# Projection pieces, heads and router products in parts between the gathered rows, and one channel block of the long convolution on GpSimd

## The chip, the cores and the metric

The kernel runs on one core of a Trainium2 chip. The metric is the device time of one execution in microseconds, the median of the runs. The core has TensorE (products into PSUM banks), VectorE, ScalarE, GpSimd (which also issues the gathers) and a queue for plain DMAs.

## What is computed

A first block and a second block over 512 tokens of width 1024, all in float32. The first block is cut here to what matters; the second (feed-forward layer, two attention mixers, feed-forward layer) follows on its result.

```python
proj = rms_norm(h, norm_mix_g) @ w_in                 # xv, bg, cg, ga, gg: 5 x 512 columns
y_sc = bg * causal_depthwise_conv(cg * xv, w_conv)    # width 3
u    = causal_depthwise_conv(ga * sigmoid(gg), w_dw) + b_dw   # width 31, 512 channels
y_cf = silu(layer_norm(u, ln_g, ln_b))
h    = h + concat(rms_norm(y_sc), rms_norm(y_cf)) @ w_out
hn   = rms_norm(h, norm_ffn_g)
q    = (hn @ w_q).reshape(512, 8, 256)
s1, s2 = q[..., :128] @ keys[:, 0].T, q[..., 128:] @ keys[:, 1].T   # 8 heads, 128 + 128 scores
# 16 best of each, 16 best of their sums: idx (one of 16384 experts) and gates (softmax), per token and head
h    = h + sum over 8 heads and 16 experts of gelu(u[idx] . hn) * gate * v[idx]
```

The last line reads 512 x 128 expert rows, each 1024 values of u and 1024 of v.

## The kernel before, in words

Tokens are cut in tiles of 128 (tile 0, and "the rest", 384 tokens, REST). The program of each engine is written out by hand, and semaphores order them.

**Prelude.** Tile 0 goes alone through projection, convolutions, output projection and hn (TensorE lines 795 to 831). Then head 0 of the router gives its list (route(0), line 1955), and the rows begin.

**Rows.** The experts are read in 512 "rows" of 1 MB: GpSimd issues for row i one gather into pair[i % 7] (NPAIR is 7, line 2834); VectorE forms the dot products (dot, 2011), ScalarE the weight and a diagonal matrix of it (weigh, 2679), and TensorE adds the weighted v (add_pair, 919, two rows at each odd i below 256) into a bank. v_used then frees the buffers, for which gather i + 7 waits (row_used, 573). The first four buffers' uses are special: gathers 3 to 6 wait for pieces 1, 3, 5 and 7 of the rest's projection, whose weights lie in their buffers. Below row 256 the tokens are arranged as 64 tokens x 2 experts, so each list is permuted by TensorE (permute, 783: indexes and gates in one bank) and copied back by VectorE (lists_back, 1999) before its rows; list r is found at rows up to TOP_ROW[r], permuted at PERM_ROW (TOP + 3) and copied at BACK_ROW (TOP + 5).

**Between rows.** Every engine has generators that yield the row at which a step is due (Paced, 313); the loop calls `until(i)` once a row, behind that row's own work on TensorE, VectorE and ScalarE and ahead of the gather on GpSimd. So the rest is computed beside the gathers: 20 projection pieces (rest_in, 719, eight products of 384 columns each; PIECE_ROW names the row of each), tile 0's heads 2 to 7 (head_q and head_S; Q_ROW), the long convolution, 30 fused multiply-adds of 384 columns for each of four channel blocks on VectorE (conv 1285, pump 1401: two taps at each row with i % 16 >= 4), the output projection from row 56, mean and variance at MEAN = 80 and VAR = 84, hn of tiles 1 to 3 up to row 115, and the router for them in nine calls (call, 896; CALL_ROW), each of sixteen products of 384 columns (128 or 256 for two of them) in one block, and six for the scores.

From row 264 the second block's first half (chain A, paced by clock) runs between the rows; chain B, for tiles 2 and 3, runs alone after row 511. Weights come in pieces of 1 MB into three slots, in the order of ORDER; each waits for the last product of the piece three before it. A bank's next use waits until its previous one is read (fresh, 671, on the counts that Plan lays out; `perm` is bank 1).

## Time and profile before

| | us |
|---|---|
| median of 3 runs | 2448.38 |
| lowest, highest | 2442.33, 2451.57 |
| profiled execution | 2457.3 |
| its span, first to last instruction | 2455.4 |
| TensorE busy | 2063.0 (84%) |
| VectorE busy | 1775.5 (72%) |
| ScalarE busy | 1174.0 (48%) |
| GpSimd busy | 729.2 (30%) |
| mean granted TensorE clock | 0.907 |

Busy time is a sum over stages with different limits, so the stretches are read one by one. A timeline row gives the start and the length of an instruction or of several alike (xN); in brackets stands how long its engine was idle before, and whom it waited for. Each float32 product of TensorE leaves two records. "POOL" is GpSimd, "DVE" VectorE, "ACT" ScalarE, "PE" TensorE.

### The profile page before, as it was taken

To read this page: it belongs to the slowest core of one execution; us is meant where nothing else is said; L and a number is where in the kernel's file an instruction comes from. 1 tells how busy PE (TensorE), PEld (TensorE's weight loads), DVE (VectorE), ACT (ScalarE), POOL (GpSimd) and SP (SyncE) were. 2 spreads that over 40 slices of the span, in tenths; PEclk is the share of its full clock that TensorE was granted. 3 is DMA by queue.
4 is the path that set the end of the run, shared out by engine and by line. 5 is a ranking of instruction groups with operands and counts; after the bars stand their busy time and mean duration, and the time that the engine had idled before them with its cause. 6 is when DMAs were issued, how large, how long until landed. Compare 5 with 4: busy or idle time off the path is not lost. (4 is left out here: it accounts for less than half of the span.)

```text
span 2455.4 us, 29687 instructions
## 1 busy us (share of the span) xinstructions
PE 2063.0 (84%) x9896; PEld 1423.4 (58%) x9896; DVE 1775.5 (72%) x3485; ACT 1174.0 (48%) x3850; POOL 729.2 (30%) x637
## 2 busy tenths in 40 slices
PE   8888886878875556999794678599989999999999
PEld 7544432334331112886343467388639988898997
DVE  6568885556668888888888998866666656656564
ACT  4345455654545556343345655433344435444443
POOL 0123343433343435233356553433320001100000
PEclk9999988889897777999896689799999999999999
DMA  9179999789889999999999999999995554124554
GB/s 363 66 288 389 368 382 376 296 333 369 341 335 383 400 408 406 383 393 421 419 398 367 374 412 420 421 394 419 420 383 189 189 167 171 69 96 162 173 188 137
DMA packets 109768, 777.73 MB, mean 317 GB/s; under 512 B 12320, under 2 KB 13088, under 8 KB 16688
## 3 DMA queue, kind: packets, MB, share of 16 engines
q0 software_dynamic: 73728, 536.90, 54.5%
q1 hardware_dynamic: 35888, 238.93, 25.7%
q8 instruction: 79, 1.29, 0.2%
q14 instruction: 73, 0.60, 0.1%
HBM read 773.69 MB, written 2.10 MB: 316 GB/s over the span
## 5 line engine op out<-in xcount | busy, mean ns | idle before, releaser
L2834 POOL DMA_INDIRECT pair<-in_uv,idx x512 | 610.0, 1191 | 921.1 <-DVE resid L1259 484.3
L2106 ACT ACTIVATE smalls<-smalls 128x1 f32<-128x1 f32 (+1 forms) x2058 | 540.5, 286 | 678.8 <-DVE smalls L2018 658.1
L664 PE MATMUL bank<-pair,diag 128*64 128x512 f32 (+1 forms) x1056 | 338.9, 760 | 208.8 <-ACT diag L2106 207.6
L2018 DVE CUSTOM_DVE_ANT_0 pair<-pair,hd 128x1024 f32<-128x1024 f32 x256 | 311.7, 1221 | 122.0 <-DMA pair<-in_uv,idx 118.7
L664 PE MATMUL bank<-ft,raw 128*128 128x256 f32 x1664 | 372.3, 386 | 11.9 <-DVE ft L1253 11.9
L664 PEld LDWEIGHTS bank<-ft,raw 128*128 128x128 f32 x1664 | 322.3, 195 | 57.7 <-issue 12.6
L2018 DVE CUSTOM_DVE_ANT_0 pair<-pair,hn 128x1024 f32<-128x1024 f32 x256 | 312.5, 1221 | 57.7 <-DMA pair<-in_uv,idx 56.8
L664 PEld LDWEIGHTS bank<-pair,diag 128*64 128x64 f32 (+1 forms) x1056 | 80.4, 163 | 421.6 <-ACT diag L2106 299.6
L1259 DVE SCALAR_TENSOR_TENSOR resid<-pair,smalls,resid 128x1024 f32<-128x1024 f32 x243 | 311.0, 1280 | 0.7 <-ACT smalls L2106 0.6
L1253 DVE TENSOR_TENSOR half<-raw,half 128x1024 fp32r<-128x1024 f32 (+2 forms) x184 | 212.0, 1191 | 122.7 <-ACT half L2106 121.2
L2106 ACT ACTIVATE half<-raw 128x1024 fp32r<-128x1024 f32 (+2 forms) x184 | 179.5, 1023 | 90.9 <-PE bank L664 90.8
L664 PE MATMUL bank<-ft_hi,half 128*128 128x256 f32 x960 | 176.5, 284 | 1.5 <-DVE ft_early L1253 1.5
L664 PE MATMUL bank<-raw,hidden 128*128 128x512 f32 x352 | 151.4, 592 | 0.0
L664 PEld LDWEIGHTS bank<-ft_hi,half 128*128 128x128 f32 x960 | 149.6, 190 | 1.9 <-issue 1.8
L2106 ACT ACTIVATE smalls<-smalls,gat 128x1 f32<-128x1 f32 x512 | 143.1, 280 | 0.0
L664 PE MATMUL bank<-ft_late_hi,half 128*128 128x256 f32 x704 | 127.5, 284 | 2.3 <-DVE ft_late_lo L1253 2.3
L2739 POOL TENSOR_TENSOR smalls<-smalls,mh 128x1 f32<-128x1 f32 (+1 forms) x21 | 18.1, 864 | 357.9 <-DVE smalls L1256 357.7
L664 PE MATMUL bank<-ht,raw 128*128 128x128 f32 (+2 forms) x512 | 117.9, 391 | 2.7 <-ACT scores L2106 2.3
L664 PEld LDWEIGHTS bank<-raw,hidden 128*128 128x128 f32 x352 | 66.9, 190 | 83.3 <-issue 83.2
L664 PE MATMUL bank<-half,hidden_hi 128*128 128x512 f32 x352 | 110.8, 395 | 1.6 <-DVE half L1253 1.6
L664 PEld LDWEIGHTS bank<-ft_late_hi,half 128*128 128x128 f32 x704 | 109.6, 190 | 2.6 <-issue 2.5
L664 PEld LDWEIGHTS bank<-ht,raw 128*128 128x128 f32 x512 | 81.7, 201 | 48.8 <-issue 20.4
(327 smaller groups left out, 3183.3 us busy)
## 6 DMA issues: line engine op xcount, KB each, us to landing
raw<-in_wts SPq DMA_DIRECT2D x201, 1024.0 KB
pair<-in_wts SPq DMA_DIRECT2D x10, 1024.0 KB, 11.0
pair<-in_uv,idx POOLq DMA_INDIRECT x512
raw<-in_wts SPq DMA_DIRECT2D x10, 512.0 KB
raw<-in_wts SPq DMA_DIRECT2D x4, 720.0 KB
resid<-in_x SPq DMA_DIRECT2D x4, 512.0 KB, 11.7
out<-resid SPq DMA_DIRECT2D x8, 256.0 KB, 5.8
raw<-in_wts SPq DMA_DIRECT2D x2, 768.0 KB
```

Source lines behind the costliest of these rows:

```text
L664: return e.matmul(o, a, b, start=start, stop=stop)
L1253: return e.tensor_tensor(o, a, b, op)
L1259: return e.scalar_tensor_tensor(out=o, in0=a, scalar=s, in1=b, op0=op0, op1=op1)
L2018: e.tensor_tensor_reduce(b[:, 0:1024], b[:, 0:1024], x_, 1.0, 0.0, ALU.mult, ALU.add, actv[:, i % 8:i % 8 + 1]).then_inc(dotted, 1)
L2106: return e.activation(o, i, f, **kw)
L2739: e.tensor_tensor(nrs[0:n, c:c + 1], nqs[0:n, c:c + 1], mh[0:n, 0:1], ALU.pow).then_inc(n_rs, 1)
L2834: e.indirect_dma_start(pair[i % NPAIR], None, uv, bass.IndirectOffsetOnAxis(ap=idx[:, n % SLOTS, k:k + 1], axis=0)).then_inc(pairs_in[i % ...
```

## The change

**Pieces and heads in halves.** rest_in(n, part) does four of the eight products; PIECE_ROWS gives each half its row. head_q takes one or both of its halves, at rows Q_ROW and Q_ROW + 1, and head_S follows at Q_ROW + 3. Head 2 moves from before row 0 to rows 7, 8 and 10. Pieces, heads and the rest become three generators of their own on TensorE, heads one on ScalarE.

**Calls in quarters.** A call's sixteen products are issued four at each of four rows; its scores follow at CALL_ROW + 5. Four calls start one or two rows earlier.

**Prelude.** Piece 0 goes in halves around the mean's column sum; the cf part's mean is taken off and squared ahead of the sc part; pieces 1, 2 and 3 are placed later; on VectorE rest_u(0) and the taps (26 before, 8 now) come after hn.

**Permutation.** Indexes and gates are permuted by two calls, each with its own use of bank 1, and VectorE copies each back with one instruction of 128 partitions in place of two of 64.

**Convolution.** VectorE does three of the four channel blocks. GpSimd does the last: for each of 30 taps a product into rstdr and an addition, one operation a row from row 16 to row 75.

**Order of weights.** Piece sc2 comes before head 3's.

```diff
-ORDER = ([(k, 2048) for k in [("wq", 1), ("wq", 2), ("sc", 0), ("sc", 1), ("wq", 3), ("sc", 2), ("sc", 3), ("bg", 0), ("wq", 4),
+ORDER = ([(k, 2048) for k in [("wq", 1), ("wq", 2), ("sc", 0), ("sc", 1), ("sc", 2), ("wq", 3), ("sc", 3), ("bg", 0), ("wq", 4),
...
-PIECE_ROW = [0, 0, 0, 0, 0, 1, 2, 3, 8, 11, 14, 16, 22, 25, 28, 31, 34, 37, 42, 45]
-Q_ROW = {3: 19, 4: 39, 5: 48, 6: 69, 7: 74}
+PIECE_ROWS = [(1, 1), (1, 3), (3, 3), (5, 5), (9, 9), (11, 11), (13, 15), (15, 17), (17, 19), (23, 25), (25, 27), (29, 29),
+              (31, 33), (35, 35), (39, 41), (43, 43)]
+Q_ROW = {2: 7, 3: 21, 4: 37, 5: 47, 6: 69, 7: 74}
...
-CALL_ROW = [104, 118, 124, 129, 136, 142, 150, 158, 166]
+CALL_ROW = [104, 118, 124, 129, 134, 142, 149, 157, 165]
...
-    p.add("perm", [1] * 16)
+    p.add("perm", [1] * 32)
...
-            def rest_in(n):
+            def rest_in(n, part):
...
-                o, done = fresh("R", n)
-                for kt in range(8):
-                    ins = mm(o[:, 0:REST], w[:, kt, j * P:(j + 1) * P], XTR[:, kt, :], kt == 0, kt == 7)
-                ins.then_inc(done, 1)
+                b = B["R", n]
+                if part == 0:
+                    fresh("R", n)
+                for kt in range(4 * part, 4 * part + 4):
+                    ins = mm(bank[b.bank][:, 0:REST], w[:, kt, j * P:(j + 1) * P], XTR[:, kt, :], kt == 0, kt == 7)
+                if part:
+                    ins.then_inc(full[b.bank], 1)
...
-            def head_q(c):
+            def head_q(c, parts=(0, 1)):
...
-                o, done = fresh("q1", c)
-                for s in range(2):
+                b = B["q1", c]
+                for s in parts:
+                    if s == 0:
+                        fresh("q1", c)
                     for kt in range(8):
-                        ins = mm(o[:, s * P:(s + 1) * P], w[:, kt, s * P:(s + 1) * P], HT[:, 0, kt, :], kt == 0, kt == 7)
-                ins.then_inc(done, 1)
+                        ins = mm(bank[b.bank][:, s * P:(s + 1) * P], w[:, kt, s * P:(s + 1) * P], HT[:, 0, kt, :], kt == 0, kt == 7)
+                    if s:
+                        ins.then_inc(full[b.bank], 1)
...
+            def permute(r, m):
+
+                e.wait_ge(gated if m else routed, r + 1)
+                src = gat[:, r % SLOTS, :] if m else ixf[r % 2]
+                o, done = fresh("perm", 2 * r + m)
...
+                    for c in range(2):
+                        ins = mm(o[64 * c:64 * c + 64, 8 * j:8 * j + 8], idt[:, 64 * j:64 * j + 64],
+                                 src.rearrange("p (q e) -> p e q", e=2)[:, c, :], True, True)
...
+            for n in (8, 9):
+                taken(e, "norm0", n)
+            rest_in(0, 0)
             e.wait_ge(late_in, 96)
             e.wait_ge(keys_in, 16)
-            taken(e, "norm0", 8)
-            taken(e, "norm0", 9)
-            rest_in(0)
             e.wait_ge(taps_done, 4)
             colsum("mean", 0, [YT0[:, 4 + ct, :] for ct in range(4)], P)
+            rest_in(0, 1)
+            e.wait_ge(sq_wide, 1)
+            colsum("var", 0, [wide0[0][:, ct * P:(ct + 1) * P] for ct in range(4)], P)
             e.wait_ge(y_hi, 4)
             y_out("ysc", 0, first_weights(10).rearrange("p (k n) -> p k n", k=4), lambda k: YT0[:, k, :], 0)
             e.wait_ge(sq_wide, 2)
-            colsum("var", 0, [wide0[0][:, ct * P:(ct + 1) * P] for ct in range(4)], P)
             mean_squares("ms", 0, [wide0[1]])
             y_out("ysc", 1, first_weights(11).rearrange("p (k n) -> p k n", k=4), lambda k: YT0[:, k, :], 0)
-            rest_in(1)
+            e.wait_ge(sq_wide, 3)
+            mean_squares("mc", 0, [wide0[1]])
             e.wait_ge(y_hi, 8)
             y_out("ycf", 0, first_weights(12).rearrange("p (k n) -> p k n", k=4), lambda k: YT0[:, k, :], 4)
             y_out("ycf", 1, first_weights(13).rearrange("p (k n) -> p k n", k=4), lambda k: YT0[:, k, :], 4)
-            e.wait_ge(sq_wide, 3)
-            mean_squares("mc", 0, [wide0[1]])
-            rest_in(2)
+            rest_in(1, 0)
+            rest_in(1, 1)
...
-            permute(0)
-            head_q(2)
-            head_S(2)
-            rest_in(3)
+            permute(0, 0)
+            rest_in(2, 0)
+            permute(0, 1)
+            rest_in(2, 1)
+            rest_in(3, 0)
+            rest_in(3, 1)
+
+            def pieces():
+
+                for n in range(4, 20):
+                    for part in range(2):
+                        yield PIECE_ROWS[n - 4][part]
+                        rest_in(n, part)
+
+            def heads():
+
+                for c, row in Q_ROW.items():
+                    yield row
+                    head_q(c, (0,))
+                    yield row + 1
+                    head_q(c, (1,))
+                    yield row + 3
+                    head_S(c)
...
+                        if kt % 4 == 0:
+                            yield CALL_ROW[c] + 2 * s + kt // 4
...
-                yield CALL_ROW[c] + 3
+                yield CALL_ROW[c] + 5
...
-            between = Paced(rest())
+            strands = Paced(pieces()), Paced(heads()), Paced(rest())
...
                     if row == i:
-                        permute(r)
-                between.until(i)
+                        for m in range(2):
+                            permute(r, m)
+                for strand in strands:
+                    strand.until(i)
...
+            centred(0, YT0[:, 4:8, :], P)
...
-            taps = [conv(YTR[:, 4 + ct, :], upadr, "cf", 31, ct, 0, REST, 9 + ct, taps_done) for ct in range(4)]
+            taps = [conv(YTR[:, 4 + ct, :], upadr, "cf", 31, ct, 0, REST, 9 + ct, taps_done) for ct in range(3)]
...
-            rest_u(0)
...
-            pump(10)
...
             mean_of("hn", 0)
-            pump(2)
             row_out(0)
-            pump(14)
+            rest_u(0)
+            pump(8)
...
-                        taken(e, "perm", n - 2)
+                        taken(e, "perm", 2 * n - 4)
...
+            def lists_back(r, m):
+
+                o, out_ = filled(e, "perm", 2 * r + m)
+                e.tensor_copy((gat if m else idx)[:, r, :].rearrange("p (q j) -> p q j", j=2),
+                              o[:, 0:16].rearrange("p (j q) -> p q j", j=2)).then_inc(out_, 1)
...
-                            lists_back(r)
+                            for m in range(2):
+                                lists_back(r, m)
...
+            taken(e, "mean", 0)
+            act(wide0[0].rearrange("p (c n) -> p c n", c=4), YT0[:, 4:8, :], ACT.Square).then_inc(sq_wide, 1)
...
-            e.wait_ge(sq_wide, 1)
+            e.wait_ge(sq_wide, 2)
             for ct in range(4):
                 gained(YT0[:, ct, :], "g_sc", ct)
-            taken(e, "mean", 0)
-            act(wide0[0].rearrange("p (c n) -> p c n", c=4), YT0[:, 4:8, :], ACT.Square).then_inc(sq_wide, 1)
             taken(e, "var", 0)
...
-            rest_gate(0)
-            rest_tap(0)
...
                 for s in range(2):
+                    yield CALL_ROW[c] + 2 + 2 * s
...
             row_turned(0)
+            rest_gate(0)
+            rest_tap(0)
             head_q(0)
             head_S(0)
             doubled(0)
             head_q(1)
...
-                        taken(e, "perm", n)
+                        taken(e, "perm", 2 * n + 1)
...
-            head_q(2)
-            head_S(2)
...
+            def last_conv():
+
+                acc, w0 = YTR[:, 7, :], COLS["cf"][0] + 3 * 31
+                yield 16
+                e.wait_ge(first_tap, 12)
+                for j in range(1, 31):
+                    if j > 1:
+                        e.wait_ge(p_step, 2 * j - 2)
+                    e.tensor_scalar(rstdr, upadr[:, 3, j:j + REST], colt[:, w0 + j:w0 + j + 1], 1.0, ALU.mult, ALU.mult).then_inc(p_step, 1)
+                    yield 15 + 2 * j
+                    e.wait_ge(p_step, 2 * j - 1)
+                    e.tensor_tensor(acc, acc, rstdr, ALU.add).then_inc(p_step if j < 30 else taps_done, 1)
+                    yield 16 + 2 * j
...
-            first, between = Paced(chain("A")), Paced(rest())
+            first, strands = Paced(chain("A")), (Paced(last_conv()), Paced(rest()))
...
-                        e.wait_ge(permuted, 3 * n + 2)
+                        taken(e, "perm", 2 * n)
```

## Rows read from the trace of the kernel before

**Rows 1.** The page: DMA busy tenths in 40 slices of the span
```profile
DMA  9179999789889999999999999999995554124554
```

**Rows 2.** Busy time by stretch, all engines, granted clock, DMA share and rate
```profile
core 0: us, PE busy (x) PEld busy (x) DVE busy (x) ACT busy (x) POOL busy (x), PEclk, DMA share, GB/s
160.00:400.00 240.00, 204.51 (x823) 94.49 (x824) 190.72 (x416) 124.53 (x490) 96.90 (x85) 0.89 0.97 387
400.00:530.00 130.00, 90.88 (x344) 36.69 (x344) 85.60 (x191) 78.51 (x275) 52.40 (x49) 0.82 0.83 324
530.00:590.00 60.00, 53.06 (x218) 28.39 (x216) 28.24 (x69) 31.16 (x123) 21.62 (x21) 0.94 0.82 320
590.00:727.00 137.00, 108.20 (x456) 51.71 (x452) 92.48 (x257) 68.14 (x274) 49.04 (x48) 0.90 0.90 354
727.00:960.00 233.00, 131.49 (x389) 32.44 (x386) 196.27 (x529) 135.31 (x560) 105.93 (x95) 0.76 0.99 397
960.00:1840.00 880.00, 736.75 (x2777) 524.68 (x2775) 719.74 (x1183) 393.00 (x1534) 360.79 (x295) 0.89 0.99 402
```

**Rows 3.** The same view of line 2018 alone, the dots
```profile
160.00:400.00 240.00, 91.35 (x149) 0.89 0.97 387
...
590.00:727.00 137.00, 49.33 (x81) 0.90 0.90 354
```

**Rows 4.** Timeline of TensorE: start, length, engine, line, operation [idle before <-releaser]
```profile
87.12 5.41 PE L664 MATMUL bank<-xt_rest,pair 128*128 128x384 f32 x16
...
94.09 1.09 PE L684 MATMUL bank<-idt,hn 128*128 128x128 f32 x8 [1.56 <-DVE hn L1259]
...
163.98 3.66 PE L664 MATMUL bank<-pair,diag 128*64 128x512 f32 x8 [9.58 <-ACT diag L2106]
...
167.44 0.39 PE L664 MATMUL bank<-smalls,idt 128*64 128x16 f32 x8
...
182.61 1.94 PE L664 MATMUL bank<-pair,diag 128*64 128x512 f32 x8
```

**Rows 5.** Timeline of VectorE from 93 to 162 us
```profile
93.95 9.12 DVE L1259 SCALAR_TENSOR_TENSOR yt_rest<-upad_rest,colt,yt_rest 128x384 f32<-128x384 f32 x14
...
103.17 0.29 DVE L1930 MAX8 vals<-scores 128x8 f32<-128x128 f32 x1
...
146.29 1.23 DVE L2018 CUSTOM_DVE_ANT_0 pair<-pair,hd 128x1024 f32<-128x1024 f32 x1 [4.82 <-DMA pair<-in_uv,idx]
...
158.59 1.23 DVE L2018 CUSTOM_DVE_ANT_0 pair<-pair,hd 128x1024 f32<-128x1024 f32 x1 [9.42 <-DMA pair<-in_uv,idx]
...
161.09 1.23 DVE L2018 CUSTOM_DVE_ANT_0 pair<-pair,hd 128x1024 f32<-128x1024 f32 x1
```

**Rows 6.** Timeline of GpSimd from 114 to 153 us
```profile
114.20 0.28 POOL L2798 TENSOR_SCALAR gat<-gat,sm 128x16 f32<-128x16 f32 x1
...
116.34 1.19 POOL L2834 DMA_INDIRECT pair<-in_uv,idx  x1 [1.86 <-DVE gat L2006]
...
140.42 1.21 POOL L2834 DMA_INDIRECT pair<-in_uv,idx  x1 [11.45 <-PE bank L664]
...
152.81 0.94 POOL L2834 DMA_INDIRECT pair<-in_uv,idx  x1 [11.18 <-PE bank L664]
```

**Rows 7.** Timelines of TensorE, GpSimd and VectorE at one call
```profile
642.95 11.76 PE L664 MATMUL bank<-ht,raw 128*128 128x384 f32 x32
...
656.86 0.94 POOL L2834 DMA_INDIRECT pair<-in_uv,idx  x1 [10.42 <-PE bank L664]
...
661.10 0.38 DVE L2006 CAST idx<-bank 64x16 uint32<-64x16 f32 x2 [8.35 <-remote]
```

**Rows 8.** Timeline of all engines at 363 us
```profile
363.37 1.22 DVE L2018 CUSTOM_DVE_ANT_0 pair<-pair,hd 128x1024 f32<-128x1024 f32 x1
...
363.39 2.40 POOL L2798 TENSOR_SCALAR gat<-gat,sm 128x16 f32<-128x16 f32 x1
```

**Rows 9.** Groups by shape: GpSimd, busy us and mean ns of one
```profile
L2763 POOL TENSOR_TENSOR smalls<-smalls,mh 128x8 f32<-128x8 f32 x20 | 38.1, 1914 | 73.7 <-DVE smalls L1256 73.5
```

More of the change, by code:

```diff
@@ L890, in rest @@
                 turned_rows("hn", "hn", 3, HN[3])
-                yield 115
-                doubled(1)
+                for j in range(2):
+                    yield 115 + 2 * j
+                    doubled(1, j)
                 for c in range(1, len(CALLS)):
@@ L2063, in vector @@
                         if row_ == i:
-                            lists_back(r)
+                            for m in range(2):
+                                lists_back(r, m)
                     between.until(i)
@@ L2582, in call, with heads @@
                 for s in range(2):
[L2583 removed]
+                    yield CALL_ROW[c] + 6 + s
                     o, out_ = filled(e, "S3", 2 * c + s)
                     act(S[:, a:b_, 2 * h + s, :], o[:, 0:n].rearrange("p (t n) -> p t n", t=b_ - a), ACT.Copy).then_inc(out_, 1)
[L2587 to L2595 removed]
+            def heads():
+                for c, row in Q_ROW.items():
+                    yield row + 2
+                    head_q(c)
+                    yield row + 4
+                    head_S(c)
+            def rest():
                 for ct, due in ((1, 0), (2, 4), (3, 6)):
@@ L2608, in rest @@
                     rest_sc_tap(ct)
-                yield from singles(33, 52)
                 yield 53
@@ L2619, in rest @@
                     gained(YTR[:, ct, :], "g_sc", ct)
-                yield from singles(52, 80)
                 yield MEAN + 3
@@ L2698, in scalar @@
             gates(0)
-            head_q(2)
-            head_S(2)
-            first, between = Paced(chain("A")), Paced(rest())
+            first, strands = Paced(chain("A")), (Paced(heads()), Paced(rest()))
             for n in range(32):
@@ L2718, in scalar @@
                         final_row(n // 8 - 1)
-                    between.until(i)
+                    for strand in strands:
+                        strand.until(i)
                     first.until(clock(i))
@@ L2809, in rest @@
                         rate("hn", t)
+            def last_conv():
[10 more added lines that the diff above has]
+                    yield 16 + 2 * j
             e.wait_ge(padded, 4)
             gates(0)
-            first, between = Paced(chain("A")), Paced(rest())
+            first, strands = Paced(chain("A")), (Paced(last_conv()), Paced(rest()))
             for i in range(PAIRS):
@@ L2816, in pool @@
                 first.until(clock(i - 8))
-                between.until(i)
+                for strand in strands:
+                    strand.until(i)
                 for r in range(1, SLOTS):
```

75 lines of the change are left out of this document (13 added, 62 removed).

## Prediction

> **What bounds the kernel now.** I read the timeline in slices first. The DMA line [rows 1] is low in slices 2 and 3 (61 to 184 us), has 7s and 8s among its 9s up to slice 12 (737 us), only 9s up to slice 30, and 1s to 5s after. Then the stretches [rows 2] and the dot products in two of them [rows 3], of which each row of pairs leaves two records. Between 727 and 960 us, and between 960 and 1840 us, the DMA engines are 0.99 busy at 397 and 402 GB/s: the gathers of 1 MB each, with the weights in between, set the pace, and what the rows gain before 727 us is carried to the end as it is, since no later stretch up to 1840 us has idle time that could take it up. After 1840 us the second chain runs alone, and the change leaves it as it was. So the change is worth what it moves before 727 us. There the DMA share is 0.97 (160 to 400), 0.83, 0.82 and 0.90 (590 to 727) [rows 2], and low before 160 us [rows 1].
>
> The gathers wait there for TensorE. A pair buffer comes free when TensorE has added two rows (1.94 us at 182.61 [rows 4]); there are seven. A router product of 11.76 us stands in front of that, GpSimd has nothing to issue for 10.42 us, and VectorE waits 8.35 us for its permuted list behind the same product [rows 7]. At 400 to 530 us the limit is the chain through ScalarE, VectorE and TensorE from MEAN to the later rows of hn. The change moves none of it.
>
> **Until the first gather.** Before the transposes of hn (94.09 us) stands the third projection piece, 5.41 us, and 1.56 us of idle time [rows 4]. The piece goes behind the first row's router; a half of piece 0 and the two column sums fill the wait for the squares. I take the transposes as 6.6 us earlier. From there to the first route() it was 103.17 - 94.09 = 9.1 us, which would be 96.6 us. But rest_u(0) and eight taps now stand before it on VectorE, behind ScalarE's gate and first tap: 8 taps of 9.12 / 14 = 0.65 us are 5.2 us [rows 5], behind the turned rows (some 2 us after 87.5) and the gate with what hangs on it (3 us, an estimate: five steps of about one tap's 0.65 us). That gives 97.7 us, so route(0) starts 5.5 us earlier, and with it the first gather (116.34 us before [rows 6]), or up to 8 us, as ScalarE has less before the gates of that list.
>
> **Rows 0 to 22.** This lead is spent again. Gather 5 waits for piece 5, gather 6 for piece 7, because their buffers hold the projection's weights. Before, piece 7 ran ahead of the addition of rows 4 and 5. Gather 5 left at 140.42 and gather 6 at 152.81 us, and each dot followed 5.9 and 5.8 us behind its gather [rows 5, 6]. Now piece 7 stands at row 5, behind add_pair(4), which needs gather 5. From my start: the list is out at about 107, and pieces 2 and 3 with the two permutations (2 x 5.4 + 2 x 0.4) hold TensorE to 118.8; dot 1 stands behind rest_u(1), which needs piece 3, so it begins at 120, and add_pair(0) 2.9 us later, at about 123 (to 125); pieces 4 and a half of 5 (8 us) to 133; add_pair(2) to 135; the other half to 137.6, gather 5 leaves at 137.9 (2.5 us earlier); dot 5 at 143.8; add_pair(4) 3 us later (dot 7 at 161.09, its addition at 163.98 [rows 4, 5]) and 1.94 long, to 148.8; piece 7 to 154.2; gather 6 at 154.5, dot 6 at 160.4 us against 158.59. So row 6 is 1.8 us late. Besides, chunk sc2 now waits for head 2, which went to rows 7 and 8: 1 MB leaves the idle time before 160 us for a stretch that is full, 1 MB / 400 GB/s = 2.6 us, of which the next stretches' idle 3% can take some. Term: **+3 us** (-5, if piece 7 doesn't hold gather 6, to +7).
>
> **Rows 8 to 80, 160 to 400 us.** 149 / 2 = 74.5 rows in 240 us are 3.22 us a row [rows 3]. At 402 GB/s in place of 387 it would be 231 us, so halves can bring 9 us at most. Many halves meet again at one odd row (15, 17, 25), where TensorE still holds 5.3 us between additions. I take -3.
>
> Two costs stand against it. The first is a new wait. Both parts of a permutation use bank 1, and the second part waits until VectorE has copied the first. VectorE does so at row TOP+5, while TensorE stands at row TOP+3. Behind that wait on TensorE lie the pieces and heads of these rows and add_pair(TOP+4), and for this wait the gathers. TensorE spent 0.39 us on a part (167.44 us) [rows 4] and went on. Now it stands still for up to two rows less the time it is behind, 0 to 5 us, five times here. TensorE is busy for 204.5 of 240 us [rows 2], and 5 x 3 = 15 us of its 35 idle us go. I take 0.6 us each on the end, +3 (0 to +15). The copies become two where there were four: less than a microsecond of VectorE for each list, hidden in its idle time.
>
> The second is the convolution on GpSimd: 60 operations of 384 columns in rows 16 to 75, one ahead of each gather. The trace has none of this size. The lower bound is VectorE's own 0.65 us for a fused tap, or less for the single product; the upper one GpSimd's 1.91 us for a power of 128x8 [rows 9]; its product of 128x16 takes 0.28 us [rows 6]. I take 0.8 us, nearer to the tap, as it is arithmetic of the same width. A row on GpSimd is then 1.19 (gather at 116.34 [rows 6]) + 0.30 + 0.8 = 2.3 us of 3.22: hidden, if nothing holds it. But the same product of 128x16 took 2.40 us when it began 0.02 us behind a dot of VectorE [rows 8]: it was held 2.1 us. And VectorE would be held by an operation of GpSimd in turn. VectorE is busy 190.7 / 74.5 = 2.56 us a row, some three quarters of it in dots and taps with two operands in SBUF; 0.75 x 0.8 adds 0.6, to 3.16 of 3.22. The relief (30 taps, 19.5 us) comes late: two taps are still pumped in each such row, the list only ends some 10 rows earlier, where DMA is full. I take +3 (-4, if the relief counts, to +20). Sum of this stretch: **+3 us**.
>
> The Trainium skill has a rule on this: by SBUF — State Buffer, section "Who interferes with whom", a VectorE instruction with two SBUF inputs and a GpSimd instruction that reads SBUF exclude each other for their whole length. The 2.40 us agree with it. By GPSIMD Engine Reference, section "Elementwise — side-by-side cycle accounting", a two-input operation takes about 2.6 cycles an element, which for 384 at 1.2 GHz is an estimate of 0.83 us; the sum by it is the same.
>
> **400 to 530 us.** Nothing but a tap list that is long done, and head 6 and 7 in halves: **0** (-3 to +2).
>
> **530 to 590 us.** TensorE is busy for 53.1 of 60 us with three calls, so 7 us is the most: **-3** (-6 to 0).
>
> **590 to 727 us, the calls.** 81 / 2 = 40.5 rows in 137 us. 354 GB/s, against 402 later: 137 x 354 / 402 = 121, so 16 us can go. With quarters (2.7 us) at four rows TensorE holds at most 5.3 us between two additions. A buffer's round (5.9 us to the dot, 2.9 from it to the addition, 2.6 for its partner row, 1.94, 1.2 for the issue) is 14.5 us, seven rows at 2.6 are 18.2, so 3.7 us are slack: nearly all of the stall goes. The new wait falls here once in eight rows, five times, when TensorE is behind anyway; at 0.6 us each it takes 3. Term: **-13** (-19 to -4).
>
> **Sum.** +3 +3 +0 -3 -13 = -10 us. The profiled execution took 2457.3 us (span 2455.4), 8.9 us over the median of 2448.38. 2457.3 - 10 = 2447.3, and on the median 2438.4, taken as **2438 us**, with 2428 to 2449 for this case alone.
>
> **Rivals.**
> - Quarters and halves give all they can. The waits on copies and ports hide, and the lead at the start is kept. -5 (head), -6 (160 to 400), -4, -16 = -31 us: 2417 us. For it: TensorE has 15% idle time at 160 to 400 us, GpSimd 60% [rows 2]. Against it: gather 6 hangs on piece 7 by the program's own order.
> - The calls' gain is lost again: TensorE stands at the permuted lists for its whole two rows, 5 us in each eight rows. Its 108.2 us at 590 to 727 plus 25 us are 133 of 137: gain 4 instead of 13 there, +3 more before: 2450 us. Nothing is measured that excludes it.
> - Slower: GpSimd and VectorE take turns at the port. A held operation, 2.1 us as in [rows 8], makes GpSimd's row 1.49 + 0.8 + 2.1 = 4.4 us in place of 3.22 in the rows with taps on both (some 33 from row 16 to 60): 33 x 1.17 = 39 us on the sum without its port term: 2474 us. It decides from where an operation and its hold exceed 3.22 - 1.49 = 1.73 us. Against it: with 20% of VectorE idle not each operation meets a chain. The page named above has this as its rule.
> - The change does what it says; the work on TensorE and its bytes stay the same, so I give that no chance of its own.
>
> **How the numbers follow.** Forecast 0.42, all gains 0.27, gain lost 0.16, port 0.15. A measurement of this kernel can tell about 0.5%, here 12.2 us, from no change: below 2436.1 is faster. That is the second case (0.27) and the lower part of the first (0.13): 0.40. Same: 0.29 + 0.14 = 0.43. Slower: 0.15 and 0.02 of the tail of the third: 0.17. The likeliest case is inside "same", near its edge. The range goes from 2412, which holds most of the second case, to 2462, which leaves out the port case.
>
> **What would show it.** Right: the hole of 10 us in GpSimd's issue at the calls is gone, the DMA share at the calls is 0.97 or more, the last of these rows is 13 us closer to the first. Dot 6 is at about 160 us although the first gather is before 112. TensorE waits for VectorE's list copy some 15 times. Operations on yt_rest on GpSimd take about 0.8 us when free. Wrong: these over 1.7 us on the mean; dots in rows 16 to 76 over 3.4 us apart; dot 6 before 156 us; or a loss after 727 us, which I put at nothing.

## The result, and the profile after

The changed kernel took 2478.18 us (median of 4 runs, 2474.92 to 2481.25), the kernel before 2449.98 us beside it: a ratio of 1.0111, with a 95% interval of 1.0093 to 1.013. It is slower by 28 us; the forecast was 2438 us, and the range ended at 2462. The profiled execution of after took 2474.92 us (span 2473.1), 3.3 us under its median; that of before took 2457.3, 7.3 us over its own. So the two traces differ by 17.6 us of span where the medians differ by 28.2. Some 5 us of before's surplus lie in rows 176 to 208, which take 89.6 us in that one trace and 83 to 88 in the others. The experiments below ran beside the kernel before, not beside the kernel after, so a distance from after is given by the medians or by the ratios, and the two differ by up to 8 us.

The busy time by stretch, for after; it answers to [rows 2]:

```profile
core 0: us, PE busy (x) PEld busy (x) DVE busy (x) ACT busy (x) POOL busy (x), PEclk, DMA share, GB/s
160.00:400.00 240.00, 192.98 (x790) 93.07 (x790) 204.47 (x372) 114.49 (x448) 156.02 (x142) 0.89 0.91 357
400.00:530.00 130.00, 91.91 (x368) 39.34 (x368) 76.33 (x161) 76.61 (x271) 48.96 (x47) 0.86 0.87 349
530.00:590.00 60.00, 46.03 (x172) 20.23 (x172) 33.05 (x83) 30.13 (x116) 21.64 (x21) 0.89 0.81 309
590.00:727.00 137.00, 111.53 (x470) 57.14 (x468) 90.29 (x242) 68.08 (x274) 54.12 (x51) 0.95 0.91 350
727.00:960.00 233.00, 133.36 (x442) 35.52 (x441) 194.72 (x530) 139.10 (x577) 103.83 (x96) 0.77 1.00 403
```

Between 160 and 400 us the DMA share fell from 0.97 to 0.91, and VectorE is busy for 204.5 us where it was 190.7, although it has a quarter fewer taps to do. The dot products alone ("dots", VectorE's instruction for one row), beside [rows 3] (two records a row):

```profile
160.00:400.00 240.00, 101.45 (x136) 0.89 0.91 357
590.00:727.00 137.00, 48.99 (x80) 0.95 0.91 350
```

There are 68 rows in the 240 us, not 74.5, and their dots take 101.5 us where 74.5 took 91.4: VectorE's own instruction became longer.

Read by the start of each row's dot (after less before, in us), the loss has places. Row 121 (532.5 us before, 554.7 after) stands at +22.2; in the kernel before, 400 us is row 81, 530 us row 120, 590 us row 135 and 727 us row 176.

| at row | 0 | 5 | 8 | 16 | 40 | 80 | 112 | 128 | 136 | 144 | 176 | 208 | end |
|---|---|---|---|---|---|---|---|---|---|---|---|---|---|
| after - before | -9.7 | -1.1 | +5.1 | +9.5 | +23.1 | +23.3 | +22.2 | +18.5 | +27.0 | +28.7 | +20.1 | +13.9 | +17.6 |

**The start.** GpSimd's gathers, beside [rows 6]:

```profile
106.51 1.19 POOL L2852 DMA_INDIRECT pair<-in_uv,idx  x1 [0.83 <-DVE idx L2013]
...
139.66 0.94 POOL L2852 DMA_INDIRECT pair<-in_uv,idx  x1 [19.20 <-PE bank L664]
157.25 0.94 POOL L2852 DMA_INDIRECT pair<-in_uv,idx  x1 [16.65 <-PE bank L664]
```

The first gather is 9.8 us earlier than before (116.34), and gathers 5 and 6 wait for TensorE 19.20 and 16.65 us. What TensorE did meanwhile, beside [rows 4]:

```profile
123.22 2.89 PE L664 MATMUL bank<-pair,diag 128*64 128x512 f32 x8 [3.97 <-ACT diag L2113]
...
148.06 3.56 PE L664 MATMUL bank<-pair,diag 128*64 128x512 f32 x8 [3.51 <-ACT diag L2113]
151.55 5.43 PE L664 MATMUL bank<-xt_rest,pair 128*128 128x384 f32 x16
169.08 3.29 PE L664 MATMUL bank<-pair,diag 128*64 128x512 f32 x8 [12.11 <-ACT diag L2113]
```

Piece 7 (151.55) stands behind the addition of rows 4 and 5; the next addition waits 12.11 us for row 6.

**Rows 16 to 45.** These are the rows where the difference grows most, and GpSimd works on its channel block there. In the lines, L2822 on GpSimd is the product, L2825 the addition, and L1272 on VectorE a tap (one fused multiply-add of 384 columns). First one such place, then VectorE's groups by shape from 196 to 345 us, which is rows 16 to 56 (busy us, mean ns of one), last the dots of the kernel before from 187 to 331 us:

```profile
243.92 0.59 POOL L2822 TENSOR_SCALAR rstd_rest<-upad_rest,colt 128x384 f32<-128x384 f32 x1
...
245.59 2.22 DVE L1272 SCALAR_TENSOR_TENSOR yt_rest<-upad_rest,colt,yt_rest 128x384 f32<-128x384 f32 x2
245.73 1.01 POOL L2825 TENSOR_TENSOR yt_rest<-yt_rest,rstd_rest 128x384 f32<-128x384 f32 x1
...
248.88 1.26 DVE L1272 SCALAR_TENSOR_TENSOR yt_rest<-upad_rest,colt,yt_rest 128x384 f32<-128x384 f32 x2
...
257.70 2.44 DVE L2023 CUSTOM_DVE_ANT_0 pair<-pair,hd 128x1024 f32<-128x1024 f32 x1
258.05 1.00 POOL L2825 TENSOR_TENSOR yt_rest<-yt_rest,rstd_rest 128x384 f32<-128x384 f32 x1
```

```profile
L2023 DVE CUSTOM_DVE_ANT_0 pair<-pair,hd 128x1024 f32<-128x1024 f32 x41 | 62.8, 1533 | 0.0
L1272 DVE SCALAR_TENSOR_TENSOR yt_rest<-upad_rest,colt,yt_rest 128x384 f32<-128x384 f32 x57 | 40.8, 716 | 1.0
...
L1269 DVE TENSOR_SCALAR pu<-pu 128x16 uint32<-128x16 uint32 x6 | 5.5, 960 | 0.1
L1266 DVE TENSOR_TENSOR cand<-vals 128x256 f32<-128x256 f32 x3 | 4.6, 1535 | 0.1
```

```profile
L2018 DVE CUSTOM_DVE_ANT_0 pair<-pair,hd 128x1024 f32<-128x1024 f32 x44 | 53.8, 1222 | 6.5 <-DMA pair<-in_uv,idx 6.3
```

Two taps take 1.26 us when no product or addition of GpSimd runs and 2.22 around an addition of 1.01; the dot takes 2.44 around 1.00. The mean dot is 1.53 us (1.22 before). In these 149 us no dot waits for its gather; before, the dots waited 6.3 us. VectorE has become the bound.

### The profile page after: what moved, and what is told of

Read it like the earlier page. It is cut to its first block and busy times, and to the rows that moved or that the text cites. A ratio compares the mean times of both kernels' runs of the same rounds, so it can differ in the third digit from the quotient of the medians.

```text
span 2473.1 us, 29708 instructions
## 1 busy us (share of the span) xinstructions
PE 2061.9 (83%) x9896; PEld 1424.5 (58%) x9896; DVE 1782.9 (72%) x3423; ACT 1173.4 (47%) x3850; POOL 794.1 (32%) x697
## 5 line engine op out<-in xcount | busy, mean ns | idle before, releaser
L2852 POOL DMA_INDIRECT pair<-in_uv,idx x512 | 616.4, 1204 | 880.0 <-DVE resid L1272 480.3
L664 PE MATMUL bank<-pair,diag 128*64 128x512 f32 (+1 forms) x1056 | 325.2, 732 | 204.5 <-ACT diag L2113 199.5
L2023 DVE CUSTOM_DVE_ANT_0 pair<-pair,hd 128x1024 f32<-128x1024 f32 x256 | 329.6, 1291 | 129.0 <-DMA pair<-in_uv,idx 128.5
L1272 DVE SCALAR_TENSOR_TENSOR resid<-pair,smalls,resid 128x1024 f32<-128x1024 f32 x243 | 311.0, 1280 | 0.6 <-ACT smalls L2113 0.6
L664 PE MATMUL bank<-ht,raw 128*128 128x128 f32 (+2 forms) x512 | 121.7, 393 | 11.0 <-ACT scores L2113 10.6
```

What stands on the lines that cost most here:

```text
L664: return e.matmul(o, a, b, start=start, stop=stop)
L1272: return e.scalar_tensor_tensor(out=o, in0=a, scalar=s, in1=b, op0=op0, op1=op1)
L2023: e.tensor_tensor_reduce(b[:, 0:1024], b[:, 0:1024], x_, 1.0, 0.0, ALU.mult, ALU.add, actv[:, i % 8:i % 8 + 1]).then_inc(dotted, 1)
L2852: e.indirect_dma_start(pair[i % NPAIR], None, uv, bass.IndirectOffsetOnAxis(ap=idx[:, n % SLOTS, k:k + 1], axis=0)).then_inc(pairs_in[i % ...
```

## Experiments

Ratios are to the kernel before, run beside them. "Dot differences" are as in the table above.

**1. Convolution back on VectorE**, the rest as after.

```diff
...
-            taps = [conv(YTR[:, 4 + ct, :], upadr, "cf", 31, ct, 0, REST, 9 + ct, taps_done) for ct in range(3)]
+            taps = [conv(YTR[:, 4 + ct, :], upadr, "cf", 31, ct, 0, REST, 9 + ct, taps_done) for ct in range(4)]
...
-            first, strands = Paced(chain("A")), (Paced(last_conv()), Paced(rest()))
+            first, strands = Paced(chain("A")), (Paced(rest()),)
```

> The changed kernel with one edit undone: the fourth channel block of the long convolution is back on VectorE, and GpSimd only gathers. Theory (port): rows 8 to 40, which came 18 us later than before, lose that delay, since VectorE's dots and taps no longer wait for GpSimd: about 2478 - 18 = 2460 us, the dots of these rows back from 1533 ns to about 1222 ns. Rival (TensorE waits for the list copies and for pieces that meet at one row): the edit gives nothing or makes it slower, since VectorE gets 30 taps more: 2478 to 2490 us.

Measured: 2457.14 us, 1.0039 (1.0023 to 1.0055). The differences are the same as after's up to row 16 (+10.0), then +8.2 at row 40 and +2.4 at row 80, where after has +23.1 and +23.3. The block on GpSimd costs 18 us by the ratios and 21 by the medians. By the traces 16.0 us of it fall in rows 16 to 45 (109.7 us with it, 93.7 without) and 5.4 in rows 45 to 80 (113.7 and 108.3).

**2. Sixty operations on GpSimd that nobody reads.** Convolution as in experiment 1, but at the rows of the 60 operations GpSimd runs as many whose result no one uses: once with reads of SBUF, once filling only. The cut shows the second of the two operations, in the variant that reads.

```diff
-                    e.tensor_tensor(acc, acc, rstdr, ALU.add).then_inc(p_step if j < 30 else taps_done, 1)
+                    e.tensor_tensor(rstdr, upadr[:, 3, j:j + REST], rstdr, ALU.add).then_inc(p_step if j < 30 else taps_done, 1)
```

> The kernel after with the fourth channel block of the convolution back on VectorE, but with 60 operations of 384 columns left on GpSimd at the same rows, whose results nobody reads (they read SBUF and write rstdr). Port theory (VectorE and GpSimd hold each other whenever both read SBUF): most of the 20 us that the convolution on GpSimd cost come back, 2457 + 15 to 20 = 2472 to 2478 us, with dots of VectorE at 1.5 us in rows 16 to 45. Rival, the length of the chain (the third block on VectorE, then mean and variance, wait for GpSimd's slow taps, or GpSimd's own row is too long): 2457 to 2460 us where nothing waits for the results.

> As the kernel with 60 operations of GpSimd that nobody reads, but each only fills rstdr with a constant, so that it reads nothing. Port theory: a filling operation doesn't hold VectorE's reading, 2457 to 2460 us, dots at 1.25 us. Rival, it is GpSimd's occupied queue that delays the gathers, whatever it does: as late as the kernel with reading operations, 2468 us or more.

Measured: with reads 2480.87 us, 1.0121 (1.0102 to 1.014); filling 2455.7 us, 1.0022 (1.0008 to 1.0035). The dots and GpSimd's operations, first with reads, then filling:

```profile
L2023 DVE CUSTOM_DVE_ANT_0 pair<-pair,hd 128x1024 f32<-128x1024 f32 x42 | 63.9, 1521 | 0.0
...
L2822 POOL TENSOR_SCALAR rstd_rest<-upad_rest,colt 128x384 f32<-128x384 f32 x30 | 34.6, 1152 | 1.2
L2825 POOL TENSOR_TENSOR rstd_rest<-upad_rest,rstd_rest 128x384 f32<-128x384 f32 x30 | 28.3, 942 | 0.7
```

```profile
L2023 DVE CUSTOM_DVE_ANT_0 pair<-pair,hd 128x1024 f32<-128x1024 f32 x49 | 59.8, 1220 | 9.9 <-DMA pair<-in_uv,idx 9.3
...
L2825 POOL MEMSET rstd_rest<- 128x384 f32 x30 | 13.1, 436 | 0.0
L2822 POOL MEMSET rstd_rest<- 128x384 f32 x30 | 13.0, 433 | 0.0
```

(The dots are those from 196 to 345 us, GpSimd's groups those from 160 to 420.) Nobody reads these results. TensorE's column sum at row 80 still waits for the last of the 60, but that one ends at 392.6 us, 27 us before the dot of row 80, and rows 16 to 45 alone take 105.9 us with reads and 92.7 with fills; so it is not the length of the chain. The filling takes 0.43 us where the reading ones take 0.94 and 1.15, so the pair doesn't hold the queue's time equal, and a fill as long as the reads was not run. But the dots themselves show what is lost: 1.52 us beside reads and 1.22 beside fills, as in experiment 1 without any. The loss comes with GpSimd's reads of SBUF, which lengthen VectorE's instructions with two operands there.

**3. Pieces 4 to 7 whole and early**, the rest as after.

```diff
-PIECE_ROWS = [(1, 1), (1, 3), (3, 3), (5, 5), (9, 9), (11, 11), (13, 15), (15, 17), (17, 19), (23, 25), (25, 27), (29, 29),
+PIECE_ROWS = [(0, 0), (1, 1), (2, 2), (3, 3), (9, 9), (11, 11), (13, 15), (15, 17), (17, 19), (23, 25), (25, 27), (29, 29),
```

> The changed kernel with pieces 4 to 7 whole at rows 0, 1, 2 and 3, as before the change, in place of halves at 1, 1, 1, 3, 3, 3, 5, 5. Theory (gather 6 hangs on piece 7 behind the addition of rows 4 and 5): gather 6 leaves before that addition, some 10 us earlier than at 157.25 us, and dot 8 with it; the whole 6 to 10 us faster, 2468 to 2472 us, if the delay of rows 8 to 40 stays as it is. Rival (what is won at the start is taken up by VectorE, which is fully busy in rows 8 to 40): dot 8 earlier, the end within 3 us of 2478.

Measured: 2467.03 us, 1.0099 (1.0072 to 1.0126).

```profile
107.15 1.20 POOL L2852 DMA_INDIRECT pair<-in_uv,idx  x1 [0.82 <-DVE idx L2013]
...
132.84 1.21 POOL L2852 DMA_INDIRECT pair<-in_uv,idx  x1 [11.45 <-PE bank L664]
145.23 0.93 POOL L2852 DMA_INDIRECT pair<-in_uv,idx  x1 [11.18 <-PE bank L664]
```

Gather 6 leaves at 145.23, 12 us earlier than in the kernel after, and the dot of row 8 stands at -7.5 where after has +5.1. The place is settled. How much reaches the end is not: the medians say 11 us, the ratios 3, with intervals that overlap. The 12.6 us won at row 8 are still 12.5 at row 40.

**4. Indexes and gates in one permutation again**, copied back by four instructions, the rest as after.

```diff
...
-                        for m in range(2):
-                            permute(r, m)
+                        permute(r)
...
```

> The changed kernel with the permutation as before: indexes and gates in one use of the bank, four copies back, no wait of TensorE for VectorE's first copy. If that wait costs what the prediction took (0.6 us at each of 15 lists, of which 10 count): 2478 - 6 = 2472 us. If the rival of the prediction holds (up to 5 us each at the calls): 2455 to 2465 us. If VectorE and the port set these rows: 2478, or 3 us more for the added copies.

Measured: 2480.11 us, 1.0135 (1.0108 to 1.0163). The wait that the prediction priced at 3 us is no net cost: without it, and with two copies more a list, the kernel is not faster.

**5. The split alone; wide copies alone.** Kernel before, once with the split permutation of after, once with one use of bank 1 as before but one copy of 128 partitions for each part. The cut is of the second. It also halves the columns of the products that permute (8 for 16), and the first gather of a list waits for one copy in place of two.

```diff
-                    for k in range(2):
-                        half_ = slice(64 * k, 64 * k + 64)
...
+                    ins = e.tensor_copy(dst[:, r, :].rearrange("p (q j) -> p q j", j=2),
+                                        o[:, 32 * m:32 * m + 16].rearrange("p (j q) -> p q j", j=2))
```

> The kernel before, with one part of the change alone: indexes and gates permuted by two calls with a use of bank 1 each, and copied back by one instruction of 128 partitions each. Theory A, from the comparison of the kernels with whole calls: this part alone is a gain of some 18 us between rows 134 and 208, since the index list no longer stands behind the gates of its list; then 2449 - 15 = about 2434 us, and the five waits of VectorE and ScalarE for a permuted list behind a product go down. Theory B, the prediction's: it is a cost of 3 us (0 to 15): 2449 to 2460 us. Theory C: it helps only where the calls are shifted by the rest of the change: 2449 +-3 us.

> The kernel before, with both parts permuted in one use of the bank as before, behind the wait for list and gates, but copied back by one instruction of 128 partitions for each part (two in place of four). If the gain of the split comes from the cheaper copies, this has most of it: about 2436 us. If it comes from indexes not waiting for the gates, this has none of it: 2449 +-3 us, while the kernel with the split alone is near 2434 us.

Measured: 2449.62 us, 0.9985 (0.9971 to 1.0), and 2444.08 us, 0.9968 (0.9953 to 0.9982), beside 2452.51. The 18 us of theory A aren't there, and the split alone is no cost of 3 us either. The wide copies, with what comes with them, bring some 8 us. The second use may take part of that away again: 5.5 us by the medians, but the intervals overlap.

**6. Calls whole again, and quarters alone.** First the kernel after with the calls at their old rows in one block; then the kernel before with quarters.

```diff
...
-                        if kt % 4 == 0:
-                            yield CALL_ROW[c] + 2 * s + kt // 4
...
```

> The changed kernel with the router's calls whole and at their old rows. From row 112 to row 208 the changed kernel gained 8 us on the one before. If the quarters give that: 2478 + 8 = 2486 us. If they give the 13 us that the prediction took, and something else lost 5 there: 2491 us. If the calls' quarters cost at rows 120 to 152 and the gain came from elsewhere: 2470 to 2478 us.

> The kernel before, with only the calls changed: four products at each of four rows, the scores five rows after the start, four calls one or two rows earlier. The prediction's theory: 13 to 16 us less between rows 128 and 180, 2434 to 2437 us. Rival, from the comparison with one permutation of both parts: quarters bring some 3 us, 2446 +-3 us, because ScalarE's copies of q and the scores come later and the list of indexes with them.

Measured: 2465.73 us, 1.0087 (1.0064 to 1.011), and 2448.34 us, 0.9988 (0.9976 to 1.0001). On the kernel before, quarters gain 4 us by the medians, within the noise by the interval. In the kernel after they cost 12 us by the medians and 6 by the ratios, with intervals that overlap. The stretches of rows 128 to 136, 136 to 144 and 144 to 176, for before, after, and after with whole calls:

```profile
558.00:591.10 33.10, 28.18 (x118) 15.38 (x117) 20.11 (x52) 16.94 (x67) 12.46 (x13) 0.95 0.81 324
591.10:616.20 25.10, 20.35 (x88) 10.18 (x87) 18.31 (x53) 13.57 (x54) 7.92 (x10) 0.93 1.01 423
616.20:726.80 110.60, 86.55 (x364) 41.23 (x364) 72.92 (x204) 54.41 (x219) 39.86 (x39) 0.89 0.87 337
```

```profile
576.40:618.00 41.60, 33.66 (x124) 18.28 (x124) 19.97 (x51) 18.49 (x73) 13.16 (x13) 0.92 0.74 274
618.00:644.80 26.80, 20.98 (x84) 10.53 (x84) 17.64 (x50) 8.95 (x37) 6.38 (x7) 0.87 0.87 341
644.80:747.00 102.20, 85.34 (x376) 41.29 (x376) 71.68 (x197) 58.87 (x239) 44.60 (x43) 0.98 0.97 380
```

```profile
583.20:611.90 28.70, 23.79 (x109) 12.64 (x108) 20.02 (x51) 16.62 (x66) 11.53 (x13) 1.00 0.87 349
611.90:637.10 25.20, 19.00 (x88) 9.99 (x87) 17.96 (x51) 13.57 (x54) 9.00 (x10) 1.00 1.01 421
637.10:737.70 100.60, 83.19 (x366) 40.16 (x364) 71.60 (x196) 55.69 (x220) 39.33 (x41) 0.97 0.95 377
```

At rows 144 to 176 the kernel after has what was forecast for the quarters, DMA share 0.97 for 0.87 and 102.2 us for 110.6; but with whole calls it takes 100.6 us there. At rows 128 to 136 the kernel after loses 8.5 us, and quarters on the kernel before lose 7 (40.1 us) at the same place. One trace each says little, so here are all sixteen of this document, by what their calls are in these rows (us, lowest to highest):

| rows | whole | quarters | quarters, banks of q swapped |
|---|---|---|---|
| 112 to 128 | 50.5 to 52.7 | 45.7 to 47.6 | 48.1, 47.3 |
| 128 to 136 | 26.4 to 33.1 | 40.0 to 43.5 | 34.9, 35.6 |
| 112 to 136 | 77.7 to 84.0 | 85.7 to 90.6 | 83.0, 82.9 |
| 144 to 176 | 100.6 to 110.7 | 100.7 to 105.6 | 101.5, 102.2, 96.9, 98.7 |

(The kernels with swapped banks are those of experiments 7 to 9; the two of experiment 9 have their early calls whole and the later ones in quarters.) So the early quarters gain some 4 us before row 128 and lose 12 behind it. At rows 144 to 176 the means are 106.7 us whole (five traces) and 101.5 in quarters (eleven): some 5 us, with ranges that overlap. TensorE's waits in the kernel after, 540 to 640 us:

```profile
PE bank L664 <- ACT scores L2113: 10.6, 3, 6.9
PE bank L664 <- ACT diag L2113: 8.5, 4, 3.4
```

The first row is the same with the convolution back, with one permutation, and with quarters alone (10.6 us, 3 times, 6.9 the longest); with whole calls it is 4.3 us, in the kernel before 2.3. A call's last scores lie in bank 0 until ScalarE reads them seven rows after the start, and the first q of the next call wants bank 0 at rows 124, 129 and 134, five or six rows after the one before.

**7. The banks of q swapped**, the rest as after.

```diff
-        p.add("q3", [0, 2])
+        p.add("q3", [2, 0])
```

> The kernel after, with the first half of a call's q in bank 2 and the second in bank 0, in place of the reverse. Theory: the quarters' loss at rows 124 to 136 (41.6 us for rows 128 to 136, 33.1 before) is TensorE waiting 10.6 us in three waits, 6.9 the longest, for bank 0, which ScalarE reads last at a row after the next call has begun; with the swap these waits are gone and the kernel is 5 to 8 us faster: 2470 to 2473 us. Rival: the wait only shows where TensorE would wait anyway for GpSimd's and VectorE's chain at rows 128 to 139: 2478 +-2 us.

Measured: 2471.99 us, 1.0078 (1.0058 to 1.0097): 6 us less than after by the medians, 8 by the ratios, with intervals that just touch. The waits on the scores are gone, and rows 128 to 136 take 34.9 us in place of 41.6. TensorE now waits 5.5 us for a piece of weights instead, which doesn't show with whole calls. By the program its slot comes free with the last product of a call, which quarters put three rows later; that this is the reason was not tried:

```profile
PE bank L664 <- ACT diag L2113: 14.7, 5, 6.4
PE bank L664 <- DMA raw<-in_wts: 5.5, 1, 5.5
```

**8. The causes together.** The block back on VectorE and pieces 4 to 7 early, first with whole calls, then with quarters and the swapped banks.

> The kernel after with three things changed: the fourth channel block of the convolution back on VectorE, pieces 4 to 7 whole at rows 0 to 3, calls whole at their rows of before; the split permutation, the halves of later pieces and the new prelude stay. If the three causes add (18 us for the port at rows 16 to 45, 11 us for piece 7 behind the addition of rows 4 and 5, 9 us for quarters beside the split): 2478 - 18 - 11 - 9 = about 2440 us, and down to 2430 us, faster than both kernels. If they cover each other (each only holds gathers that another holds too, or the lead is spent before row 128): 2448 to 2456 us.

> The kernel after with the fourth channel block back on VectorE, pieces 4 to 7 whole at rows 0 to 3, calls still in quarters but q in banks 2 and 0. If quarters are worth their 8 to 9 us over rows 144 to 176 (24.0 us for eight rows at full clock, 25 to 28 us with whole calls) once their wait for the bank is gone: 2441 - 6 = about 2435 us, against 2441 us with whole calls. If the quarters gain nothing beside the split permutation: 2441 +-3 us.

Measured: 2441.04 us, 0.9958 (0.9945 to 0.997), and 2432.41 us, 0.9929 (0.991 to 0.9948). Both beat both kernels. Dot 8 stands at -8.6 and -8.5, row 40 at -3.1 and -3.3.

**9. Whole calls first, quarters later; then one use of the bank.** The kernel of experiment 8 with the calls up to row 136 whole and those from 142 on in quarters; then the same with the lists permuted in one use and copied by one wide instruction for each part.

```diff
+WHOLE = 5
...
-                        if kt % 4 == 0:
+                        if c >= WHOLE and kt % 4 == 0:
```

> The kernel with all three causes taken back (fourth block on VectorE, pieces 4 to 7 whole at rows 0 to 3, q in banks 2 and 0), with the calls at rows 104 to 136 whole as before and only those from row 142 on in quarters. If the quarters' loss lies in the calls of rows 129 and 134, where the extra calls for the hn of tiles 1 to 3 stand close together: rows 128 to 136 in 29 to 31 us in place of 35.6, rows 144 to 176 still in 103 us, the kernel 2432 - 4 = about 2428 us. If the loss comes from something later (the weights that a later last product lets in later): 2432 +-2 us, and the loss shows up in rows 136 to 160.

> As the kernel with whole calls first and quarters later, but indexes and gates permuted in one use of bank 1 and copied back by one instruction of 128 partitions each. If the second use and its wait cost what the kernels of before say (0.9985 against 0.9968): 4 us less, about 2424 us. If that was scatter: the same as the other within 2 us.

Measured: 2435.67 us, 0.9938 (0.9917 to 0.996), and 2423.4 us, 0.9899 (0.9881 to 0.9917). The first has scattered runs, 2425.74 to 2437.57, so that by the medians it is no better than the second kernel of experiment 8; its trace has the expected shape:

```profile
548.10:577.30 29.20, 23.18 (x105) 12.36 (x105) 20.17 (x52) 16.85 (x66) 14.23 (x13) 0.91 0.89 365
577.30:602.80 25.50, 21.90 (x90) 10.39 (x87) 17.93 (x50) 13.38 (x54) 8.41 (x9) 0.90 1.01 421
602.80:699.70 96.90, 81.50 (x368) 39.74 (x366) 71.13 (x197) 54.38 (x220) 40.67 (x40) 1.00 0.98 382
```

Rows 128 to 136 take 29.2 us, so their loss came from the quarters of the early calls; but rows 112 to 128 take 52.0 us where the quarters took 47.3, so together only 1.7 us are won. Rows 144 to 176 take 96.9 us. The second, with one use of bank 1, is the best kernel of the study, 1.0% faster than before and, by the medians, 2.2% faster than after. By the medians the second use of the bank costs 12 us, by the two profiled executions 4; the intervals touch at 0.9917, so the size stays open. The sign is that of experiment 5.

## Why the prediction was wrong, point by point

The terms of the sum, each at the rows that its stretch holds in the kernel before:

| term | rows | forecast | measured |
|---|---|---|---|
| the start ("rows 0 to 22") | 0 to 8 | +3 | +5.1 |
| 160 to 400 us | 8 to 80 | +3 | +18.2 |
| 400 to 530 us | 80 to 121 | 0 | -1.1 |
| 530 to 590 us | 121 to 136 | -3 | +4.8 |
| 590 to 727 us | 136 to 176 | -13 | -6.9 |

The sum was -10; the trace has +20.1 at row 176. Half of the distance is the second term. Of the signs that the prediction named for being wrong, one came: the dots of rows 16 to 76 are 211.2 / 60 = 3.52 us apart, over 3.4. Of its signs of being right, the DMA share at the calls was 0.91 and not 0.97.

**What bounds the kernel, and that a loss is carried to the end: right.** After 960 us the difference moves by 2.5 us, +15.1 at row 264 and +17.6 at the end.

**Until the first gather: right, the gain a little low.** Forecast 5.5 to 8 us earlier, measured 9.8.

**Rows 0 to 22: the mechanism right, the size low.** Gather 5 was put at 137.9 and left at 139.66, gather 6 at 154.5 and left at 157.25; dot 6 was put 1.8 us late and is 4.5 late. Two slower additions (2.89 and 3.56 us, priced at 1.94) are 2.6 of the missing 2.7 us: the granted clock was 0.63 and 0.53 in them, after TensorE had been idle for 3.97 and 3.51 us, and 1.00 in the addition at 134.67 us, 1.94 long, which followed other work. Experiment 3 shows the place. Beyond row 8 another 4.4 us go between rows 8 and 16 (forecast for sc2: some 2.6). In the kernels of experiment 8 it is 7 us between rows 12 and 16, and there VectorE waits once for 8.6 us for piece 9, behind head 2 (5.92 us) and piece 8 on TensorE: the moved head, not the transfer, is what the rows show. This was read, not tried.

**Rows 8 to 80: the step that failed.** Forecast +3, measured +18.2 (+5.1 to +23.3); the block on GpSimd alone costs 18 to 21 us (experiment 1), priced at +3. The slower rival had the cause, mutual exclusion, and the forecast had the size of an operation (0.8 us taken, 0.59 to 1.01 when free) and of what VectorE loses: 0.6 us a row was taken, and rows 16 to 45 show 101.3 - 82.6 = 18.7 us in 29 rows, 0.64 a row. What failed is the step after it: these 0.6 us were taken to vanish in VectorE's idle time. The first reason is the base to which they were added. The 2.56 us of VectorE a row was a mean over 160 to 400 us; by rows 16 to 45 alone it was 82.6 / 29 = 2.85 of 3.31 us; 2.85 + 0.64 is 3.49, over the row. The same view, cut at row 45, would have given a loss, but of 0.18 x 29 = 5 us only. The second reason is larger: of the 18.7 us more that VectorE is busy, its idle time took up 4.9 (13.3 us before, 8.4 after), and 13.8 us lengthened the rows. A row of after takes 109.7 / 29 = 3.78 us, not 3.49:

```profile
186.70:282.60 95.90, 83.86 (x339) 41.01 (x339) 82.59 (x184) 46.64 (x182) 34.81 (x32) 0.92 0.96 385
282.60:396.30 113.70, 94.33 (x392) 41.89 (x393) 81.10 (x179) 60.69 (x242) 49.88 (x43) 0.89 0.96 381
```

```profile
196.20:305.90 109.70, 92.58 (x366) 45.65 (x365) 101.33 (x180) 49.38 (x192) 69.30 (x64) 0.92 0.88 337
305.90:419.60 113.70, 87.41 (x363) 39.68 (x363) 84.33 (x162) 58.64 (x231) 74.63 (x67) 0.86 0.94 374
```

These are rows 16 to 45 and 45 to 80, of before and then of after. Against the kernel before, all of the loss lies in the first pair: 95.9 to 109.7. In rows 45 to 80 it hides a gain: without the block on GpSimd they take 108.3 us (experiment 1).

The rival's own working (GpSimd's row too long at 4.4 us) had the wrong engine: GpSimd is busy for 69.3 of 109.7 us, and VectorE decides. That its 2474 us lie near the 2478 measured is luck: its port term was 39 us where 18 to 21 are shown, and the calls that it took as a gain of 13 us gave less. The 2.1 us of hold that it took from [rows 8] were two dots in a row, 1.22 us each; the second is this line of the kernel before:

```profile
364.51 1.22 DVE L2018 CUSTOM_DVE_ANT_0 pair<-pair,hd 128x1024 f32<-128x1024 f32 x1
```

In the kernel after a product on GpSimd is held for 0.54 us on the mean (0.59 free, 1.13).

The rule of the Trainium skill, SBUF — State Buffer, section "Who interferes with whom", that a VectorE instruction with two inputs in SBUF and a GpSimd instruction that reads SBUF contend, holds here for both sides: two taps grow by 0.96 us around an addition of 1.01, and a product on GpSimd by these 0.54 us. From the Trainium skill, GPSIMD Engine Reference, section "Elementwise — side-by-side cycle accounting", the prediction estimated the addition at 0.83 us; it takes 1.01.

**The wait at the permuted lists: right that it exists, wrong that it matters as priced.** From 187 to 440 us TensorE waits for it 6.5 us in 4 times (from 160 to 727 us 14.1 us in 11, with some 15 forecast); experiment 4 shows no gain without the split, and experiment 5 no loss with the split alone. But the prediction counted the copies' saving as hidden. With one use of the bank and half as many copies the kernel before gains 0.32%. A copy takes 0.17 us with 64 partitions as with 128, so 0.35 us a list goes, 5 us over 15 lists if none of it was hidden; whether the 8 us come from there, from the narrower products or from the earlier first gather of a list isn't settled.

**400 to 530 us: right.** Forecast 0, measured -1.1.

**530 to 727 us, the calls: the second step that failed.** Forecast -3 and -13, measured +4.8 and -6.9. Up to row 128 the quarters do gain (-3.7 us over rows 112 to 128), and rows 144 to 176 give -8.6 us and share 0.97; but experiment 6 puts only some 5 us of these to the quarters. What failed is that quarters were checked against buffers, not against banks: stretched from three rows to five, a call overlaps the next one's bank 0, +8.5 at rows 128 to 136. Experiment 7 shows it: the swap takes the waits away and 6.7 us from these rows. The clock may also take part: whole calls took 100.6 us for rows 144 to 176 at a granted clock of 0.97, 106.9 at 0.94, 107.0 at 0.92, 108.1 at 0.90 and 110.6 at 0.89, so a part of the 16 us that "can go" may belong to neither form; what sets the clock there was not tried, nor which of the two is the cause.

## What to carry to other kernels

Price a load moved to another engine on the narrowest stretch in which it runs, not on the mean of a stretch twice as long: 2.85 of 3.31 us a row has no room for 0.64, and 2.56 of 3.22 seemed to. And don't let added time fill an engine's idle time before you have found what that time waits for: here the idle time took up 4.9 us of 18.7. Work given to GpSimd beside a VectorE that reads two operands from SBUF was not moved here, it was added: 60 operations cost some 20 us, and as fills that read nothing, none. When a step is stretched over more rows, follow every buffer and bank that it holds to its next user, and every piece of weights that is ahead of a buffer's release.

## What the runs showed of the hardware

A dot can lose more than the addition lasts. In rows 16 to 56 of the kernel after, ten dots have an addition of 1.01 us that starts 0.24 to 0.35 us behind them by the profile; they take 2.35 to 2.46 us in place of 1.22, and the addition isn't lengthened. Why it is 1.22 us and not 1.01 is not shown.

Small VectorE instructions are held as well. The sum of 128x256 takes 0.43 us alone and 1.54 on the mean beside GpSimd's convolution. The integer TENSOR_SCALAR of 128x16 takes 0.17 us alone and 0.96 on the mean there; of the six, three take 1.76 us, each around an addition, and three 0.16. Beside fills that read nothing, where dots and taps were untouched, the integer instruction took 0.42 us:

```profile
L1272 DVE SCALAR_TENSOR_TENSOR yt_rest<-upad_rest,colt,yt_rest 128x384 f32<-128x384 f32 x68 | 41.9, 617 | 1.2
...
L1269 DVE TENSOR_SCALAR pu<-pu 128x16 uint32<-128x16 uint32 x6 | 1.4, 418 | 0.1
```
